# An expert's weights with four neighbouring rows on each partition instead of rows 128 apart

## The reference, cut to what matters

```python
def _moe(h, router_w, router_b, w_gate, b_gate, w_up, b_up, w_down, b_down):
    logits = (h @ router_w + router_b).astype(jnp.float32)
    top_logit, top_e = lax.top_k(logits, TOP_K)
    top_w = jax.nn.softmax(top_logit, axis=-1)
    ...
    def expert_block(args):
        xe, e = args
        gate = jnp.minimum(xe @ w_gate[e] + b_gate[e], SWIGLU_LIMIT)
        up = jnp.clip(xe @ w_up[e] + b_up[e], -SWIGLU_LIMIT, SWIGLU_LIMIT)
        act = (up + 1) * (gate * jax.nn.sigmoid(SWIGLU_ALPHA * gate))
        return act @ w_down[e] + b_down[e]
```

## Time and profile before

| | |
|---|---|
| median of three runs | 2151.24 us (2149.73 to 2152.42) |
| the profiled execution: device time | 2153.75 us |
| its span in the trace | 2151.9 us |
| mean granted TensorE clock over the span | 0.967 |
| expert loop, first gate matmul to the last down matmuls | 490.7 to 1472.6 us |

### The profile page before, as it was taken

One profiled execution on the slowest core, in us unless ns is written; L12 is line 12 of the kernel. 1 busy time (PEld: TensorE's weight loads), 2 busy tenths in 40 slices (PEclk: granted clock), 3 DMA queues, 4 the chain that ended last, 5 costly groups with the idle time before them and its releaser, 6 DMA issues.

```text
span 2151.9 us, 25550 instructions
## 1 busy us (share of the span) xinstructions
PE 1971.6 (92%) x10893; PEld 1278.5 (59%) x10893; DVE 671.5 (31%) x1259; ACT 544.2 (25%) x971; POOL 13.1 (1%) x48
## 2 busy tenths in 40 slices
PE   3999977979999999999999999996999998989999
PEld 2776645864444434443444444443878998778998
DVE  0123232221122212221221122114455455655544
ACT  1311331121111101101110111013545444555443
POOL 1000000000000000000000000000000000000000
PEclk9999988979999999999999999997999999999999
DMA  9521403627999999999999999995533554523641
GB/s 309 191 78 62 173 1 137 235 84 289 409 409 409 409 409 409 409 409 409 409 409 409 409 409 409 408 407 188 192 118 128 185 177 157 196 79 118 197 168 66
DMA packets 199157, 563.53 MB, mean 262 GB/s; under 512 B 7200, under 2 KB 55328, under 8 KB 199040
## 3 DMA queue, kind: packets, MB, share of 16 engines
q1 hardware_dynamic: 194160, 557.86, 67.7%
q10 hardware_dynamic: 4880, 3.99, 0.6%
HBM read 560.78 MB, written 1.05 MB: 261 GB/s over the span
## 4 chain that ended last, share of the span: by engine, by line
PE 64%; DMA 26%; DVE 4%; ACT 2%; ACTq 1%; issue 1%; SPq 0%; DVEq 0%
DMA ring<-in_w_up 26%; PE ps L879 13%; PE ps L334 11%; PE ps L946 8%; PE ps L947 8%; PE ps L948 8%; PE ps L608 3%; PE ps L900 3%; PE ps L845 1%; PE ps L573 1%; PE ps L870 1%; PE ps L990 1%; PE ps L680 1%; PE ps L580 1%; ACT arena L1227 1%
## 5 line engine op out<-in xcount | busy, mean ns | idle before, releaser
L879 PE MATMUL ps<-ring,arena 128*64 128x512 f32 x2048 | 450.4, 593 | 22.3 <-DMA ring<-in_w_up 22.3
L946 PE MATMUL ps<-part,part 128*128 128x256 f32 (+1 forms) x1168 | 380.9, 326 | 5.9 <-DVE part L1665 4.5
L947 PE MATMUL ps<-part,part 128*128 128x256 f32 (+1 forms) x1168 | 376.1, 322 | 0.0
L948 PE MATMUL ps<-part,part 128*128 128x256 f32 (+1 forms) x1168 | 375.5, 321 | 0.0
L1662 DVE TENSOR_SCALAR arena<-ps 64x512 f32<-64x512 f32 (+2 forms) x133 | 90.2, 678 | 866.9 <-PE ps L879 783.3
L879 PEld LDWEIGHTS ps<-ring,arena 128*64 128x64 f32 x2048 | 155.6, 137 | 312.5 <-issue 312.5
L1665 DVE TENSOR_TENSOR part<-ring,part 128x1024 fp32r<-128x1024 f32 (+1 forms) x248 | 248.7, 1053 | 98.5 <-ACT part L1227 98.5
L900 PE MATMUL ps<-ring,arena 128*64 128x512 f32 x1024 | 231.6, 606 | 22.0 <-ACT arena L1227 22.0
L1227 ACT ACTIVATE arena<-ps 128x512 f32<-128x512 f32 (+4 forms) x231 | 112.7, 504 | 503.4 <-PE ps L900 234.9
L946 PEld LDWEIGHTS ps<-part,part 128*128 128x128 f32 x1168 | 225.0, 193 | 22.9 <-DVE part L1665 5.3
L948 PEld LDWEIGHTS ps<-part,part 128*128 128x128 f32 x1168 | 224.5, 192 | 16.6
(11 more groups left out here) (238 smaller groups left out, 1289.5 us busy)
## 6 DMA issues: line engine op xcount, KB each, us to landing
ring<-in_w_gate SPq DMA_DIRECT2D x64, 2048.0 KB, 16.6
ring<-in_w_up SPq DMA_DIRECT2D x64, 2048.0 KB, 21.3
ring<-in_w_down SPq DMA_DIRECT2D x64, 2048.0 KB, 17.8
ring<-in_ffn_w_in SPq DMA_DIRECT2D x44, 1024.0 KB, 7.8
ring<-in_w_ada SPq DMA_DIRECT2D x12, 2048.0 KB, 13.7
ring<-in_ffn_w_out SPq DMA_DIRECT2D x10, 2048.0 KB, 7.7
ring<-in_w_in SPq DMA_DIRECT2D x8, 2048.0 KB, 11.2
ring<-in_a_w_in SPq DMA_DIRECT2D x6, 2048.0 KB, 11.8
```

Of the source, the lines that this page charges most:

```text
L879: i = e.matmul(PS[p + h][CAP * r:CAP * r + CAP, :], xg[:, k0 + k, :], W(w[r])[:, k, 512 * h:512 * h + 512], start=False, stop=k0 == 4 and ...
L946: e.matmul(out, x[0], y[0], start=first, stop=False, skip_group_check=True)
L947: e.matmul(out, x[0], y[1], start=False, stop=False, skip_group_check=True)
L948: return e.matmul(out, x[1], y[0], start=False, stop=last, skip_group_check=True)
```

## The change

The six loads of an expert use a new function `plan_rows`: partition p gets rows 4p to 4p + 3 of the piece of 512 rows, which are 16 KB in one run both in HBM and in SBUF. A contraction tile k of a piece then holds the rows 4c + k. The other operand of each matmul is put in the same order: ScalarE's four copies to `b.htok` read PSUM with a step of four elements, and VectorE's multiply by the sigmoid writes its result in that order, into the gate plane of `gus` (elements 4c + k go to 128k + c), where the transposes now read. The second branch gets 16 transposes and four copies ahead of its loop and reads its gate and up weights with a step of four; it isn't run with these inputs. The host lays the biases of that branch out accordingly.

```diff
+        def plan_rows(key, w, k0):
+
+            src = w[128 * k0:128 * k0 + 512, :].rearrange("(p k) n -> p k n", k=4)
+            plan(key, 4, D, lambda ap: [(ap, src)])
+
...
         for ex in range(NE):
             for k0 in (0, 4):
-                plan_cols(("moe_g", ex, k0), A["w_gate"][0][ex], 0, 1024, k0, 4)
-                plan_cols(("moe_u", ex, k0), A["w_up"][0][ex], 0, 1024, k0, 4)
+                plan_rows(("moe_g", ex, k0), A["w_gate"][0][ex], k0)
+                plan_rows(("moe_u", ex, k0), A["w_up"][0][ex], k0)
             for k0 in (0, 4):
-                plan_cols(("moe_d", ex, k0), A["w_down"][0][ex], 0, 1024, k0, 4)
+                plan_rows(("moe_d", ex, k0), A["w_down"][0][ex], k0)
...
+        def in_fours(x):
+
+            return x.rearrange("p (c k) -> p k c", k=4)
...
-                            i = e.transpose(PS[p][:, CAP * j:CAP * j + CAP], gus[:, 1, 128 * j:128 * j + 128],
+                            i = e.transpose(PS[p][:, CAP * j:CAP * j + CAP], gus[:, 0, 128 * j:128 * j + 128],
                                             C("ident", CAP, CAP))
...
-                copy(b.htok[:, q, 512 * g:512 * g + 512], PS[n]).then_inc(*s_htoke.up(n))
+                copy(b.htok[:, q, 512 * g:512 * g + 512].rearrange("p (k c) -> p k c", k=4), in_fours(PS[n])).then_inc(*s_htoke.up(n))
...
-                        tt(u, u, sg, ALU.mult).then_inc(*s_act.up(ex, h))
+                        tt(g.rearrange("p (k c) -> p c k", k=4), u.rearrange("p (c k) -> p c k", k=4),
+                           sg.rearrange("p (c k) -> p c k", k=4), ALU.mult).then_inc(*s_act.up(ex, h))
```

More of the change, by code:

```diff
@@ L375, in build @@
         s_moe = signal("experts_done")
+        s_dht, s_dh = signal("dense_h_turned"), signal("dense_h_evicted")
         late = ringt[:, 4:6, :].rearrange("p s n -> p (s n)")
@@ L906, in tensor_program @@
             with e.Else():
+                for n in range(4):
+                    if n:
+                        e.wait_ge(*s_dh.of(n - 1))
+                    for j in range(2):
+                        for q in range(2):
+                            i = e.transpose(PS[1][:, 256 * j + 128 * q:256 * j + 128 * q + 128],
+                                            b.htok[:, q, 128 * (2 * n + j):128 * (2 * n + j) + 128], C("ident"))
+                    i.then_inc(*s_dht.up(n))
+                e.wait_ge(*s_dh.of(3))
                 for ex in range(NE):
@@ L919, in tensor_program @@
                             for k in range(KT):
-                                i = e.matmul(PS[1 + n % 3][:, T * r:T * r + T], W((kind, ex, 4 * (k // 4)))[:, k % 4, 128 * f:128 * f + 128],
+                                i = e.matmul(PS[1 + n % 3][:, T * r:T * r + T], in_fours(W((kind, ex, 4 * (k // 4)))[:, k % 4, 512 * (f // 4):512 * (f // 4) + 512])[:, f % 4, :],
                                              b.h2[:, k, :], start=k == 0, stop=k == 7, skip_group_check=True)
@@ L1431, in scalar_program @@
             with e.Else():
+                for n in range(4):
+                    e.wait_ge(*s_dht.of(n))
+                    copy(b.h2[:, 2 * n:2 * n + 2, :], PS[1].rearrange("p (j n) -> p j n", j=2)).then_inc(*s_dh.up(n))
                 for ex in range(NE):
@@ L2231 @@
     put("b_ada", _np.repeat(cols(I["b_ada"][0]), 2, axis=1))
-    put("b_gate", cols(I["b_gate"][0].reshape(-1)))
-    put("b_up", cols(I["b_up"][0].reshape(-1)))
+    for n in ("b_gate", "b_up"):
+        put(n, I[n][0].reshape(64, 128, 4).transpose(1, 0, 2).reshape(128, 256))
     put("norm_mix", cols(I["norm_mix_2"].reshape(-1)))
```

## The result

The changed kernel takes 2157.02 us (median of 8 runs, 2155.09 to 2161.02) against 2150.32 of the kernel before (2148.67 to 2152.42): ratio 1.0031, 95% interval 1.0022 to 1.0040. Run a second time it stood at 1.0016 (1.0007 to 1.0025). So it is slower by 3 to 7 us. The forecast was 2149.0: 2.2 us less than the 2151.24 that it was set beside, with "slower" at 0.28. The profiled execution took 2158.3 us, its span is 2156.5.

What follows compares the result with a forecast made beforehand. The prediction took the expert loop to be paced by DMA at 30.7 us an expert against TensorE's 29.74. Terms -28.9 + 12.5 + 13.6 + 0.6 = -2.2 gave 2149 us beside the median; range 2125 to 2175, likeliest case 2141 to 2155.

Steps and rivals of the forecast that it cites:

- Term 1: Expert loop's loads: 16 KB packets bring the DMA's pace under TensorE's, so waits for the up load go: -28.9 us.
- Term 2: VectorE's multiply before the transposes: its stepped write makes each expert 0.38 us longer: +12.5 us, bounds 0 and 24.5.
- I take 1.00 us: VectorE's multiply with the stepped write: assumed duration, against 683 ns contiguous, so +0.32 us, twice for each expert.
- slack of 0.25 us: Before the fifth transpose in each expert: delay the second multiply can take without holding TensorE up, some 0.25 us.
- Term 3: TensorE's down matmuls: more idleness before them drops the granted clock in more experts, 1.7 us each: +13.6 us.
- I take one in four, 8: Down matmuls of the expert loop: assumed number of additional clock falls, bounds one more or all 31.
- Term 4: ScalarE's four copies to `b.htok` ahead of the loop: stepped PSUM reads cost +0.6 us (0 to 2.4).
- third rival: Expert turn: longer multiply takes the DMA's place; 1.28 us ends the gain, 1.40 us gives 2175; chance 0.20.
- Number 1: Expert loop: clock falls only one to three times, multiply at 1.0 us: 2138 us; chance 0.18.
- Number 2: VectorE's multiply: stepped write costs nothing, 683 ns, TensorE keeps 29.74 us an expert: 2127 us; chance 0.14.
- Number 4: Expert loads: packets stay at 4 KB or are no faster, DMA pace stays 30.7 us: 2152 us; chance 0.05.
- Number 5: Down matmuls: clock falls in nearly every expert, 53 us instead of 13.6: 2188 us; chance 0.06.

Runs made afterwards that it cites:

- Number 2: Changed kernel with the down loads, multiply and transposes back in their old form, only gate and up in 16 KB runs: 2128.01 us, ratio 0.9889 to the kernel before.
- number 10: Changed kernel plus two unread 128-column matmuls filling only TensorE's wait ahead of the down matmuls: 2139.71 us, ratio 0.9944 to the kernel before.
- number 6: Changed kernel with unread matmuls in both TensorE waits, 64 columns before the second four transposes: 2140.48 us, ratio 0.9949 to the kernel before.
- number 8: Changed kernel with the second down piece back in rows 128 apart, so only the first half's multiply steps: 2127.70 us, ratio 0.9893 to the kernel before.
- number 5: Kernel before plus only the stepped multiply and the transposes' gate plane, old loads kept: 2153.81 us, ratio 1.0012 to the kernel before.
- number 1: Changed kernel with a contiguous in-place multiply and transposes reading with a step of four instead: 2154.24 us, ratio 1.0015 to the kernel before.

## Why the prediction was wrong, step by step

**Term 1, the loads: right.** Packets of 16 KB, the DMA under TensorE's pace, no wait for the up load. Number 2 shows the gain nearly by itself: -23.5 us, with down still in 4 KB rows and two inner falls (3.4 us). And with the inner falls taken away only terms 1 and 2 are left, -28.9 + 16.2 = -12.7; the measured differences are -13.4 (number 10) and -10.5 (number 6).

**Term 2, the multiply: right in kind, too small.** The step of the prediction that failed is "I take 1.00 us". The slack of 0.25 us was confirmed by number 8. The multiply was put at 1.00 us and takes 1.051, so an expert gets 2 x 0.368 - 0.25 = 0.49 us longer (measured 0.50), not 0.38. With the last expert, 31 x 0.50 + 0.7 = 16.2 us instead of 12.5. The Trainium skill's 1.71 ns a column for a destination that hops 4 KiB at each element (Vector Engine (DVE) Microarchitecture Reference, section 5.2) is close to the measured 1.01 + 0.72 = 1.73 for a hop of 512 bytes; its other price, 2.50, is not. Which of the two would hold was open before the run.

**Term 3, the clock: right in kind, too small.** The step that failed is "I take one in four, 8", at 1.7 us. There were ten inside the loop, one in three, at 1.45 to 1.7 us each, 15.4 together, and the falls of the first and last expert, which the prediction left as they were, grew by 1.4 each (10.06 and 10.03 us against 8.69 and 8.67): 18.1 instead of 13.6. That a choice between 1 and 31 came as near as 8 is luck; nothing in the trace gave the number.

**Term 4, the copies: nothing** instead of 0.6.

**The sum** with measured terms: -28.9 + 16.2 + 18.1 = +5.4 us against the -2.2 forecast; the two profiled executions differ by 4.6, the medians by 6.7 and, in the second measurement, by 2.9. The sign was decided by 3.7 us in the one term and 4.5 in the other, each a small part of its term, because a gain of 29 stood against losses of about the same size. The forecast had 0.42 on faster and 0.28 on slower; the point was 6 to 8 us too low. What failed is the size of terms 2 and 3, not the mechanism. The third rival had the limit: with 8 falls it put the end of the gain at a multiply of 1.06 us, and 1.051 with ten falls lies beyond the end.

**The rivals.** Number 1 (few falls, 2138) was not what happened. With the inner falls taken away by filling, the time is 2140.5 and 2139.7, near its 2138, in part because its multiply is too cheap by 3.7 us and it still counts 3 us of falls. Number 2 (no cost of the write) and number 3 (1.28 us and more) are out by the multiply's 1.051. Number 4 said that with old packets 0.38 us would hide in the wait for the up load; number 5 shows that it would not have hidden as told, since the falls came there as well and took the wait's place. Number 5 (a fall in nearly every expert) is out: every third.

**What stays open.** Filling shows that the idle 0.69 us has a part in the falls. Why they come in just every third expert isn't settled. In number 1 (30.19 us) the expert with a fall is longer than its neighbours by 1.5 to 1.6 us, in the changed kernel (30.24) by 1.45 to 1.7, and from one fall to the next three experts take 92.1 to 92.4 us in both, so the length of an expert and the price of a fall aren't independent there; that this beat is worth 30.7 us an expert, the old DMA pace, looks like a coincidence, and it makes before and after come out alike. Why number 8 has no inner fall where number 2 has two isn't settled either, and with one profiled execution each it may be chance.

## What to carry to other kernels

Where a new layout moves work from one engine to another, look for the part of it that is free: gate and up took the new order for nothing (the tokens are put in it once, ahead of the loop), and down had to be paid in every expert; taking only the first part is worth 1.1%, taking both costs 0.2 to 0.3%. When a transfer stops being the bound, the next engine's turn is laid bare, with every wait in it: price those waits before, and count the clock with them. A wait on TensorE can cost more than its length; filling it with matmuls that nobody reads is a quick test of that, and here a remedy of 14 to 18 us.

## What was not expected of the hardware

- VectorE's tensor-tensor multiply with contiguous reads and a write that steps 512 bytes: 1051 ns for 64 x 512, against 683.
- ScalarE reading PSUM with a step of four floats: 596 ns for 128 x 512, no longer than contiguous.
- TensorE loading 64 x 128 weights in float32 with a step of four: 214 ns and one in 120 ns, against 139 and one in 62.
- HBM to SBUF in 16 KB packets: 631 ns of an engine each, against four of 164 ns in 4 KB packets by the same measure.
- The granted clock went to the lower level (1.2 GHz) after the turn in every third expert in five profiled executions whose turn holds waits of 0.29 and 0.69 us, or 0.69 us and slow transposes, and in none between first and last where most of the 0.69 us wait was filled.
